# Two-block transformer kernel: compression units spread through the stream, probabilities scaled on VectorE, gate halves in the attention's run-out, three bank sets for the merge, earlier splits at two joints

## What is computed

```python
h = rms_norm(x, norm1_g)
proj = h @ w_in + b_in            # q, k, v of three attentions, small gates, 3*1024 merge gates
y_a = fox_attention(qa, ka, va, fa)                 # 4 heads, forget gates
y_b = dilated_attention(qb, kb, vb, dil_slopes)     # 6 heads in 3 groups, joined by a softmax over groups
y_c = nsa_attention(...)                            # 6 heads: compressed + selected + window attention
#   compress_blocks: gelu(flat @ w1) @ w2, 15 overlapping blocks of 32 tokens, for k and for v
g = sigmoid(gates).reshape(B, S, 3, D)
merged = g[:, :, 0] * (y_a @ w_pa) + g[:, :, 1] * (y_b @ w_pb) + g[:, :, 2] * (y_c @ w_pc)
x = x + merged @ w_o
x = x + conv_ffn(rms_norm(x, norm2_g), w_up, conv_w, conv_b, w_down)
```

## Time and profile before

| | |
|---|---|
| time of the runs, median of 3 | 958.61 us (958.3 to 964.05) |
| profiled execution | 960.3 us |
| its span | 958.5 us |
| TensorE busy | 886.9 us, 93% of the span |
| VectorE / ScalarE busy | 517.5 / 485.4 us |
| GpSimd busy | 68.7 us |
| granted TensorE clock, mean | 0.977 |

### The profile page before, as it was taken

One profiled execution on the slowest core, in us unless ns is written; L12 is line 12 of the kernel. 1 busy time (PEld: TensorE's weight loads), 2 busy tenths in 40 slices (PEclk: granted clock), 3 DMA queues, 4 the chain that ended last, 5 costly groups with the idle time before them and its releaser, 6 DMA issues.

```text
span 958.5 us, 15615 instructions
## 1 busy us (share of the span) xinstructions
PE 886.9 (93%) x6286; PEld 801.6 (84%) x6286; DVE 517.5 (54%) x887; ACT 485.4 (51%) x817; POOL 68.7 (7%) x83
## 2 busy tenths in 40 slices
PE   5999699898889999989989999999989799988987
PEld 5999598787879999978779999888867699986565
DVE  4343245455655666655775343356667645546435
ACT  5652347464364544545573245466646655533433
POOL 0000002554300000000000000000000000000410
PEclk9999799899999999989999999999999899999999
DMA  8554643135343555545535234423336354533031
GB/s 310 221 217 138 229 161 120 62 128 170 132 148 133 179 183 191 192 135 186 196 127 193 91 133 161 147 88 133 133 125 215 107 180 173 176 132 119 14 110 44
DMA packets 21556, 144.55 MB, mean 151 GB/s; under 512 B 2513, under 2 KB 3153, under 8 KB 4720
## 3 DMA queue, kind: packets, MB, share of 16 engines
q1 hardware_dynamic: 20592, 140.55, 42.4%
q10 hardware_dynamic: 896, 3.03, 1.0%
HBM read 142.53 MB, written 1.05 MB: 150 GB/s over the span
## 4 chain that ended last, share of the span: by engine, by line
PE 76%; DVE 9%; ACT 8%; issue 3%; DMA 2%; POOL 2%; SPq 0%; DVEq 0%; POOLq 0%; ACTq 0%
PE PS L403 75%; DVE wl L1551 3%; ACT wh L1059 3%; DMA ring<-w 2%; POOL PB L2135 1%; ACT PB L1093 1%; ACT L1416 1%; ACT PB L1234 1%; POOL PB L2151 0%; ACT hh L1073 0%; ACT L1420 0%; DVE hl L1571 0%; PE PS L989 0%; DVE PB L1946 0%; DVE Y L1970 0%
## 5 line engine op out<-in xcount | busy, mean ns | idle before, releaser
L1551 DVE TENSOR_TENSOR wl<-ring,wh 128x1024 fp32r<-128x1024 f32 x248 | 302.9, 1227 | 343.4 <-ACT wh L1059 343.3
L1059 ACT ACTIVATE wh<-ring 128x1024 fp32r<-128x1024 f32 x248 | 260.4, 1056 | 301.1 <-PE PS L403 282.8
L403 PE MATMUL PS<-hh,wh 128*128 128x256 f32 x1244 | 361.5, 291 | 12.4 <-DVE hl L1609 5.3
L403 PE MATMUL PS<-hl,wh 128*128 128x256 f32 x1244 | 355.6, 286 | 0.0
L403 PE MATMUL PS<-hh,wl 128*128 128x256 f32 x1244 | 355.2, 286 | 0.0
L403 PEld LDWEIGHTS PS<-hh,wh 128*128 128x128 f32 x1244 | 242.4, 195 | 18.3 <-issue 8.7
L403 PEld LDWEIGHTS PS<-hl,wh 128*128 128x128 f32 x1244 | 242.5, 195 | 0.7 <-issue 0.5
L403 PEld LDWEIGHTS PS<-hh,wl 128*128 128x128 f32 x1244 | 242.3, 195 | 0.0
L403 PE MATMUL PS<-wh,hh 128*128 128x256 f32 (+2 forms) x528 | 176.9, 335 | 12.8 <-DVE hl L1571 7.6
L403 PE MATMUL PS<-wl,hh 128*128 128x256 f32 (+2 forms) x528 | 173.1, 328 | 0.0
L403 PE MATMUL PS<-wh,hl 128*128 128x256 f32 (+2 forms) x528 | 173.0, 328 | 0.0
(11 more groups left out here) (266 smaller groups left out, 721.0 us busy)
## 6 DMA issues: line engine op xcount, KB each, us to landing
ring<-w SPq DMA_DIRECT2D x128, 1024.0 KB, 4.9
cn<-consts SPq DMA_DIRECT2D x2, 1051.0 KB, 7.6
V<-gains ACTq DMA_DIRECT2D x3, 512.0 KB, 4.7
cn<-consts SPq DMA_DIRECT2D x1, 1050.5 KB, 8.7
xa<-x SPq DMA_DIRECT2D x2, 512.0 KB, 4.6
out<-xb SPq DMA_DIRECT2D x4, 256.0 KB, 2.1
cn<-late ACTq DMA_DIRECT2D x1, 704.0 KB, 6.3
cn<-conv ACTq DMA_DIRECT2D x1, 470.0 KB
```

The source lines that it names most:

```text
L403: return nc.tensor.matmul(o, lhsT, rhs, start=start, stop=stop, skip_group_check=True)
L1059: A(wh[:, q % SPLITS, :], ring[:, u % RING, e:e + HALF], ACT.Copy).then_inc(sem("hi_ready"), 1)
L1551: TTn(wl[:, q % SPLITS, :], ring[:, unit_of(q) % RING, e:e + HALF], wh[:, q % SPLITS, :].bitcast(F32), ALU.subtract).then_inc(sem("split_d ...
```

## The change

1. **Order of the stream.** `ORDER` and `PLACE` put the four cmp units singly in front of proj 11 and gates 0, 1 and 2. `w` is permuted on the host; ring slots go by the place in the order. TensorE runs `cmp_hidden` one unit at a time, and the fox rows come after the second of them. Five gate units instead of four stand before the attention.
2. **Scaling.** VectorE multiplies the probabilities (`scale_probs`) instead of GpSimd.
3. **Run-out.** One gate half in each of steps 0 to 13. Units 10 and 11 are stored so that both first parts (input tiles 0 to 3) come before both second parts. Y tiles 0 to 3 are split at step 12, tiles 4 to 7 at step 14.
4. **Merge.** Three bank sets, and the first two parts of branches 0 and 1 before their third parts.
5. **Joints.** One half instead of three is split before the first evacuation. In the last up step the first four inputs of down are split after the unit's first half is used instead of its second.

```diff
+CMP_BEFORE = {FIRST["proj"] + 11: 0, FIRST["gates"]: 1, FIRST["gates"] + 1: 2, FIRST["gates"] + 2: 3}
+ORDER = []
+for _u in range(NU):
+    if _u in CMP_BEFORE:
+        ORDER.append(CMP0 + CMP_BEFORE[_u])
+    if not CMP0 <= _u < CMP1:
+        ORDER.append(_u)
+PLACE = {u: i for i, u in enumerate(ORDER)}
+CMP_FIRST, CMP_LAST = PLACE[CMP0], PLACE[CMP1 - 1]
...
-Y_SPLIT_AT = {NP + 1: (0, 1, 2, 3), NP + 2: (4,), NP + PV_LAG - 1: (5,)}
-
-GATE_HALVES = [0] + [min(16, -(-16 * (s + 1) // (NP + 1))) for s in range(NP + PV_LAG)]
-
-FAC = [j + 1 if j < 4 else 5 if j < 10 else j - 4 for j in range(NJ)]
+Y_SPLIT_AT = {NP + 1: (0, 1), NP + PV_LAG - 1: (2, 3, 4, 5)}
+
+GATES_BEFORE = 5
+GATE_PARTS = [(u, part) for u in range(GATES_BEFORE, 10) for part in range(2)]
+GATE_PARTS += [(u, part) for part in range(2) for u in (10, 11)]
+GATE_HALVES = [min(s, len(GATE_PARTS)) for s in range(NP + PV_LAG + 1)]
...
-            def refill(u):
-
-                v_ = u - RING
+            def refill(i):
+
+                v_ = ORDER[i - RING]
                 if CMP0 <= v_ < CMP1:
...
-                nc.sync.dma_start(ring[:, u % RING, :], w[u]).then_inc(sem(f"unit_in[{u % RING}]"), 16)
+                nc.sync.dma_start(ring[:, i % RING, :], w[i]).then_inc(sem(f"unit_in[{i % RING}]"), 16)
...
-            cmp_hidden(0)
-            cmp_hidden(1)
+            for i in (9, 10):
+                wide_a(i)
+            cmp_hidden(0, 0)
+            wide_a(11)
+            cmp_hidden(0, 1)
+            fox_rows()
+            wide_b(FIRST["gates"])
+            cmp_hidden(1, 0)
             cmp_fold(0)
-            wide_b(FIRST["gates"], (0,))
+            wide_b(FIRST["gates"] + 1)
+            cmp_hidden(1, 1)
+            cmp_out(0)
+            wide_b(FIRST["gates"] + 2, (0,))
             cmp_fold(1)
-            wide_b(FIRST["gates"], (1,))
-            cmp_out(0)
-            wide_b(FIRST["gates"] + 1)
+            wide_b(FIRST["gates"] + 2, (1,))
             cmp_out(1)
-            wide_b(FIRST["gates"] + 2)
+            wide_b(FIRST["gates"] + 3)
             cmp_scores()
-            wide_b(FIRST["gates"] + 3)
+            wide_b(FIRST["gates"] + 4)
             cmp_probs()
             for s_ in range(NP + PV_LAG):
                 for q in range(GATE_HALVES[s_], GATE_HALVES[s_ + 1]):
-                    wide_b(FIRST["gates"] + 4 + q // 2, (q % 2,))
+                    u, part = GATE_PARTS[q]
+                    wide_b(FIRST["gates"] + u, (part,), half_of("gates") + 2 * GATES_BEFORE + q)
...
-                if i >= 2:
-                    pe.wait_ge(sem("branches"), i - 1)
-                o = (PS[:, 2 + 2 * (i % 2), 0:S], PS[:, 2 + 2 * (i % 2), S:2 * S], PS[:, 3 + 2 * (i % 2), 0:S])
-                for s_, (k0, k1) in enumerate(((0, 2), (2, 5), (5, 8))):
+                if i >= 3 and 0 in parts:
+                    pe.wait_ge(sem("branches"), i - 2)
+                n = 2 + 2 * (i % 3)
+                o = (PS[:, n, 0:S], PS[:, n, S:2 * S], PS[:, n + 1, 0:S])
+                for s_ in parts:
+                    k0, k1 = ((0, 2), (2, 5), (5, 8))[s_]
...
+            for i in range(2):
+                branch_part(i, (0, 1))
+            for i in range(2):
+                half_out(branch_part(i, (2,)))
+            for i in range(2, 8):
+                half_out(branch_part(i, (0, 1, 2)))
...
-            halves(SPLITS)
+            halves(1)
             act.wait_ge(sem("vecs_in"), 16)
...
             cmp_copy(0)
+            act.wait_ge(sem("fox_rows"), 1)
+            A(foxr, PS[:, SC[0], 0:S], ACT.Copy).then_inc(sem("fox_rows_copied"), 1)
+            gate(0)
+            cmp_gelu(0)
+            gate(1)
             cmp_copy(1)
-            cmp_gelu(0)
+            cmp_kv(0)
             cmp_gelu(1)
-            cmp_kv(0)
-            gate(0)
+            gate(2)
             cmp_kv(1)
-            gate(1)
-            gate(2)
+            gate(3)
 
             act.wait_ge(sem("cmp_centred"), 1)
             cm12 = cols2(CM, 12)[:, :, 0:15]
             A(cm12, cm12, ACT.Exp).then_inc(sem("cmp_exp"), 1)
-            gate(3)
+            gate(4)
...
-                unit(u)
+                multiplied(half_at(u))
                 if i == NF - 1:
 
                     act.wait_ge(*read(FIRST["up"] + DOWN_EARLY - 2))
                     act.wait_ge(*read(FIRST["up"] + DOWN_EARLY - 1))
                     for k in range(DOWN_EARLY):
                         deep_high("down", BIG, DOWN, k)
+                multiplied(half_at(u) + 1)
...
+            def scale_probs(a, b):
+
+                settled()
+                for j in range(a, b):
+                    for t in range(TT):
+                        q = PB[:, j % 8, 0:P] if t == 0 else PB[:, j % 8, P:3 * P]
+                        ins = TS(q, q, fac[:, 2 * j + t:2 * j + t + 1], None, ALU.mult)
+                    ins.then_inc(sem("probs_scaled"), 1)
...
+                    scale_probs(2 * s_ - 2, 2 * s_)
                 if s_ == 4:
                     factor(9)
-
-                halves(half_of("gates") + 8 + GATE_HALVES[s_ + 1] + SPLITS)
+                    scale_probs(4, 10)
...
-                keep_up(u)
                 if i == NF - 1:
+                    halves(half_at(u) + SPLITS + 1)
                     for k in range(DOWN_EARLY):
                         deep_low("down", BIG, DOWN, k)
+                keep_up(u)
...
-            for j in range(NJ):
-                pool.wait_ge(sem("fac_ready"), FAC[j])
-                for t in range(TT):
-                    q = PB[:, j % 8, 0:P] if t == 0 else PB[:, j % 8, P:3 * P]
-                    ins = nc.gpsimd.tensor_scalar(q, q, fac[:, 2 * j + t:2 * j + t + 1], None, ALU.mult)
-                ins.then_inc(sem("probs_scaled"), 1)
```

More of the change, by code:

```diff
@@ L1659, in _ @@
                         add_pe(nc.vector, q).then_inc(sem("flat_ready"), 1)
-            for i in range(3):
+            for i in range(4):
                 keep_up(FIRST["gates"] + i)
@@ L2305 @@
     odd_out = a["odd_w_out_2"][0]
+    gate_units = wide(w_in[:, gates], KD)
+    gate_units[10:12] = gate_units[10:12].reshape(2, P, 2, HALF).transpose(2, 1, 0, 3).reshape(2, P, UNIT)
     units = {
-        "proj": wide(w_in[:, order], KD), "gates": wide(w_in[:, gates], KD),
+        "proj": wide(w_in[:, order], KD), "gates": gate_units,
         "cmp": np.concatenate([a[n][0].reshape(2, 8, P, 256).transpose(0, 2, 1, 3).reshape(2, P, UNIT)
@@ L2321 @@
     }
-    w = np.concatenate([units[name] for name, n in STREAM])
+    w = np.concatenate([units[name] for name, n in STREAM])[ORDER]
     small = np.concatenate([w_in[:, fa], w_in[:, gc], eg], 1)
```

79 lines of the change are left out of this document (36 added, 43 removed).

## The result

| | before | after |
|---|---|---|
| median of the runs compared, us | 960.92 (958.30 to 964.05, 4 runs) | 937.61 (937.07 to 937.77, 4 runs) |
| profiled execution, us | 960.3 | 937.77 |
| its span, us | 958.5 | 935.9 |
| its mean granted clock | 0.977 | 0.979 |

The ratio is 0.9755, with a 95% interval of 0.9717 to 0.9793: 2.5% faster. The forecast was 935.0, with a range from 930 to 944. The sum of its terms was 23.6 us, and the profiled span is 22.6 us shorter. That looks like a hit on every count, and it is not: the stretches that the terms stand for gave 30.6 us, and 8.0 of them were lost again further back.

A forecast was written before the change was run, and what follows sets the result against it. TensorE, 76% of the span, bounds the kernel; idle time before its matmuls, with slow-clock matmuls behind long waits, is the gain. Terms sum to 23.6 us: profiled 960.3 becomes 936.7, median 935.0, range 930 to 944.

The forecast's parts named there:

- The start: Before the first weight matmul: one half split first cuts the 2.40 us wait to 0.1; gain 2.3, bounds 1.3 and 3.5.
- The compression: Compression units spread between wide units: old waits and slow matmuls of 10.7 us go, new waits 1.6; gain 9.1.
- what I had left open: Price of the weight loads in the compression: 4.9 us alone, 8.1 where another was under way; gain bounds 9.5 and 3.
- the gelu's: At the first cmp_out: TensorE waits 1.15 us behind ScalarE's split, read of gates 0, table load and gelu.
- the one of 0.45 at gates 0: At gates 0: chain of 7.9 us from the freed slot against cover of 7.5; wait 0.45 with the steps between.
- The scaling: First block's attention: VectorE scales at 0.38 us a job; 5.8 us of cost goes, new waits 2.25; gain 3.55.
- the run-out: Attention steps 12 to 14: a gate half each in steps 12 and 13 covers waits; gain 2.4, bounds 1.5 to 2.6.
- the small waits of the early steps: Early attention steps without turns: 4.1 us against VectorE's circle of 4.93, costing 0.65 and 0.3 us.
- The merge: Merge branches: three read waits, 2.1 us, go; a new wait of 0.85 at the first branch; gain 1.2.
- The joint: Between up and down: wait 0.75 instead of 2.91 us and the clock stays; gain 5.05, bounds 2.0 and 5.8.
- the clock falls at short waits: Rival: four waits of 0.75 to 1.3 us each bring slow matmuls worth 1.6, together 6.4; 941.4 us; chance 0.06.

The follow-up runs named there:

- the first experiment: The changed kernel with three halves split before the first evacuation, as before the change; 940.47 us.
- the kernel before with the filler: The kernel before with only four matmuls of unread output added before head 2's scores in the second block's attention; 959.94 us.
- GpSimd's scaling: The changed kernel with the first block's probabilities scaled on GpSimd again, as before the change; 936.67 us.
- the filler in both kernels: Four matmuls of unread output before head 2's scores in the second block's attention: changed kernel 933.68 us; with first-block scaling on GpSimd 937.06 us.
- the bunched units: The changed kernel with the four compression units together again, read-outs on ScalarE in their old order; 946.99 us.
- the packed halves: The changed kernel with its 14 gate halves in attention steps 0 to 11, none left for steps 12 and 13; 939.11 us.

## Why the prediction came out right, step by step

**The start** was under-sized: 4.8 us (2.1 idle, 2.7 pace) for a term of 2.3, and beyond its bound of 3.5. I had the pace in the bound only; it was the larger half. One of the 4.8 belongs to the profiled execution of the kernel before: against the first experiment, and against the kernel before with the filler, the changed kernel is 3.8 us ahead at the same matmul.

**The compression** was right: 9.7 for 9.1, and 9.9 when it was undone. The loads were slower than I had taken. Those issued from 80 to 100 us took 5.5 to 6.3 us (medians by 4 us), where I had 4.9; one of them:

```profile
ring<-w SPq DMA_DIRECT2D x1, 1024.0 KB, 6.3
```

That is part of what I had left open, up to 8.1 us. Still, not one wait for them is left in TensorE's timeline: there was more cover than I had counted. Of the two new waits the gelu's was there (0.87 for 1.15), the one of 0.45 at gates 0 was not.

**The scaling and the run-out** gave 8.0 us for 5.95. A pair of pieces takes VectorE 0.46 us from start to start at the burst (twelve in 2.75), not the 0.38 that I took:

```profile
L1780 DVE TENSOR_SCALAR PB<-PB,tiny 128x256 f32<-128x256 f32 x20 | 6.9, 347 | 0.0
L1780 DVE TENSOR_SCALAR PB<-PB,tiny 128x128 f32<-128x128 f32 x20 | 5.7, 283 | 0.3
```

(VectorE's groups by shape from 140 to 205 us.) From the fixed cost in the Trainium skill (VectorE: DVE Perf Modes, the section on the TRN2 errata) the estimate was 0.22 and 0.29 us for them. The trace agrees that there is such a cost, and measures 0.28 and 0.35 us, somewhat more. The wait was mis-sized for another reason. I had VectorE 2.5 us behind the scores of pair 4; it read them 1.8 us after they ended (148.66, 150.47). With that the first scaled job was ready 0.56 us after TensorE asked, not 1.3, and the small waits of the early steps (0.65 and 0.3) never came: being behind costs nothing before somebody waits. The run-out was worth 2.7 in the attention, for 2.4, which leaves 5.3 for the scaling's 3.55 (GpSimd's scaling made the attention 4.9 us longer in one trace and 6.2 in the other). In the whole it is worth 3.4 us with the filler in both kernels, and nothing without it (GpSimd's kernel is 0.9 us the faster, within its spread), because of the fall that it brings on in the second block. That the 3.4 lies near my 3.55 is chance.

**The merge** gave 1.9 to the start of w_o (1.6 to the first tap) for 1.2: one wait of 0.29 instead of 0.85, and 0.3 more behind the merge. That the changed order of the parts needs the third bank set I had not seen; with two sets the kernel is 4.8 us slower.

**The joint** was right in its mechanism: a wait of 0.73 for 0.75, the clock at 1.00 behind it, 2.2 and 2.9 us. Another 1.5 came in up, where the clock had been low at its start before and wasn't after; no term had it, and not every variant with the same up has it (the bunched units, GpSimd's scaling and the packed halves take 137.4 us there instead of 135.9).

**What failed** is what the sum left out. I took the idle times in front of matmuls for all there is to gain, priced the clock only where a wait went, and took the rest of the program for fixed. The second block lost 2.4 us on the way to its attention and 5.6 in it, and both are slow matmuls. The 5.6 are the change's own: the scaling on VectorE stretches a wait from 0.77 to 1.11 us, and the clock falls behind it. The 2.4 are not, they come and go between kernels with the same code there. The terms were too small by 7.0 us, and a loss of 8.0 stood in none of them; that the sum still came out at 22.6 for 23.6 is luck.

The rival *the clock falls at short waits* (0.06) was right in kind and wrong in place: the clock did fall at one of 1.11 us, in a stretch that I had taken for fixed, and did not at those of 0.87, 0.56 and 1.12 that I had forecast. My argument against it does not hold either. It was the stretch at 703 us, with waits of 1.55, 1.47 and 1.29 us and the clock at 1.00. The same three waits stand in the changed kernel up to 680.9 us, and there the clock fell with them:

```profile
680.80:684.00 3.20, 3.13 (x8) 2.49 (x9) 0.69 (x1) 0.00 (x0) 0.00 (x0) 0.50 0.03 5
```

It fell there in seven of the fourteen profiled executions of this document, and held in the other seven.

## What to carry to other kernels

Lay the two traces side by side by milestones, the same instruction in each, before believing a total: here a gain of 30.6 us and a loss of 8.0 hid in one number, and a part that is worth 3.4 us (the scaling) looked worthless. Follow a change into code that it doesn't touch: 0.35 us on one engine's queue, far behind the edit, cost 5.6. Spreading small units of the stream between large ones was worth 9.4 us here, and a reordering that finishes results later needed another buffer with it. Where a short wait can't be removed, matmuls whose output nobody reads may be cheaper than leaving it idle: four of them gave 3.9 us where the clock had fallen, and nothing in the same place where it had held.

## What the runs showed of the hardware that I had not expected

- The granted clock does not follow from the length of the wait in front of it alone. It fell to 0.50 (the 1.2 GHz level) behind 1.11 us of idle time, stayed at 1.00 (2.4 GHz) behind 1.12 us, and behind 2.9 us in one execution of a kernel that is unchanged there, where another had 0.77 over the same 15 us. But at one place the length did tell: 1.11 us brought the fall seven times out of seven, 0.76 or 0.77 us not in the two traces that have it. With work in the gap the clock stayed at 1.00 behind it in both places where that was tried. I can't say what decides it.
- Moving 44 small operations to VectorE in the first block delayed one operation of VectorE by 0.35 us some 650 us after the last of them, in all ten kernels that have them there. No trace shows why.
- The changed kernel's four executions lie within 0.7 us, the kernel before's 35 within 7.2. Four fillers in its second block did not close that spread.
- At the start of the kernel before, matmuls of 256 columns started 0.21 us apart for 6 us. The column of the granted clock says 1.00 there because the trace has no record of the clock yet.
- A scaling of 128x256 takes 0.35 us on VectorE and 0.93 to 1.06 us on GpSimd.
